# Even and odd channel tiles as the two halves of a seven-product matrix scheme, with other buffers for the first weight blocks of a layer

## Chip, cores and metric

The kernel runs on 1 core of one Trainium2 chip, as one program that takes all inputs of one inference step and writes all outputs. The metric is the device time of one execution in microseconds (us); lower is better. Before the change the median of 3 runs is 1267.34 us (1266.87 to 1272.12).

## What is computed

A trunk of two layers with width 1024 works on 544 tokens (512 of a prompt, 32 sampled) with shared weights. Layer 0 mixes by a causal convolution beside an attention, layer 1 by a chunked spatial gate; each layer then adds a squared-ReLU MLP of hidden width 4096. The change lies where a mixer's output projection ends and the MLP begins:

```python
xp = xp + merged @ wo                       # layer 0: output projection
xp = xp + mix_p                             # layer 1: (u * mix) @ w_out
xp = xp + sq_relu_mlp(rms_norm(xp, norm_ffn_g[layer]), w_ff_up[layer], w_ff_down[layer])

def sq_relu_mlp(h, w_up, w_down):
    a = jax.nn.relu(h @ w_up)
    return (a * a) @ w_down
```

All is float32.

## The kernel before

**Numbers in two parts.** Each float32 operand x is split into a rounded part "hi" and the rest "lo" = x - hi, and a product is three matmuls: hi by hi, lo by hi, hi by lo. ACT makes hi by a copy, DVE makes lo by a subtraction. Activations stand transposed: channels on the partitions, in KT = 8 channel tiles of 128, with T = 544 tokens in the free dimension, handled as two halves of HALF = 272.

**Output projection.** Eight output tiles (N_OUT = 20 to 27 in layer 0, N_OUTC = 44 to 51 in layer 1) are made by PE in function tile, 48 matmuls each, in two pairs of PSUM banks that take turns. A tile needs the lo part of its weights (lo_done) and, for its banks, the evacuation of the tile two before it (evac_done). DVE's add_to_x adds the tile to xT. The weight blocks are 256 columns wide (two tiles) and lie in two buffers of w_raw.

**Seven products for the up projection.** For a pair of hidden tiles (128 + 128 columns) the product of the 1024 channels with the tokens is treated as a product of 2 by 2 blocks: the channels are two halves (KH = 4 channel tiles each), the tokens are two halves, the hidden columns are two tiles. Seven products p1 to p7 of 12 matmuls take the place of eight. They need sums of weight blocks, which DVE makes in place (weight_sum: s1, s2, s3, s4), and sums of activation blocks: B_hi and B_lo (for p1, p2, p3, p5) and the three tiles of B_T (for p6, p7, p4). The halves are channel tiles 0 to 3 and 4 to 7.

**One layer's MLP.** The hidden width is cut into CHUNKS = 4 chunks of 1024. A chunk has 28 products (list ORDER: p1 0, p5 0, p1 1, p5 1, p2 0, p2 1, p6 0, p6 1, p7 0, p7 1, p4 0, p3 0, ...), then 16 halves of the down projection (d0, d1 for each of 8 output tiles). The weights of product q go to a ring of RING = 8 slots: ACT's weights_hi runs eight products ahead of PE, DVE's weights_lo seven. Between the products DVE also evacuates the results (part_11, part_22, part_12) and makes the lo parts of the hidden values (lo_row1, lo_row2), and ACT does relu and square. Product p6 0 waits for the evacuation of p1 0 and p2 0 by part_11 (c11_done).

**The stretch from projection to MLP.** Function to_ffn, once on ACT and once on DVE, goes through the eight output tiles j = 0 to 7. For j below 4 ACT makes B_hi of the first token half, and DVE the difference xg_f of the two token halves, from which ACT and DVE make the second half of B_hi and B_lo (p5's operand). For j of 4 and above, the operands of p6, p7 and p4 are made too: each combines channel tile j with channel tile j - 4. In the same loop come the splits of the last projection tiles (split_hi, split_lo), a running sum of squares for the norm (square_sum), the first sums of weights, and the first seven weights_lo. The norm's reciprocal, r_all, is made after the statistics in four parts (invert_part), at the products in INVERT_AT.

**What sets the order.** Every engine has one instruction queue, written by hand in the order of its block in the program, and semaphore waits between them. No scheduler moves anything. The weight loads are issued by SP (SyncE) in its own order, each behind the wait for its buffer. A block of the MLP's weights is 1 MB, loaded as two DMAs; block f of a layer goes to buffer f % 3: two buffers of w_raw, which it shares with the projections, and w_raw2, which lies where the mixer's data were.

Of the kernel before, what the change touches and what calls it, by code (L numbers as in the profile page):

```python
# [84 lines left out]
def build(nc, i, o):  # L85
# [78 lines left out]
    with ExitStack() as ctx:  # L164
# [187 lines left out]

        def raw_block(f):

            return w_raw[:, f % 3, :, :] if f % 3 < 2 else w_raw2[:, :, :]

        def raw_part(layer, c, product):

            name, u = product
            raw = raw_block(block_of(layer, c, product))  # L360
            if name[0] == "d":
                k0, col = KH * int(name[1]), P * (u % 2)
            else:
# [2060 lines left out]
```

## Time and profile before

| | before |
|---|---|
| median of 3 runs | 1267.34 us |
| the profiled execution, its own time | 1266.53 us |
| its span in the trace | 1264.8 us |
| PE busy | 1204.1 us, 95% of the span |
| DVE busy | 857.4 us, 68% |
| ACT busy | 604.2 us, 48% |
| GpSimd (POOL) busy | 64.7 us, 5% |
| chain of waits that ended last | PE 80%, DVE 11%, ACT 4%, issue 2%, DMA 1% |
[...]

How to read it: the profiled execution took 0.8 us less than the median, and 1.7 us of it lie outside the span of its instructions. A difference that is worked out in the trace is taken off 1266.53. PE is busy nearly all the time, so time can be won only where it stands or runs at the lower clock; the stretches in which it does are found in the timeline of PE by the idle time printed in brackets, with the instruction that is taken to have ended it. An instruction's printed duration holds some of its tail: where instructions follow one another without a gap, the distance from start to start is what each costs its engine.

### The profile page before, as it was taken

To read this page: it belongs to the slowest core of one execution; us is meant where nothing else is said; L and a number is where in the kernel's file an instruction comes from. 1 tells how busy PE (TensorE), PEld (TensorE's weight loads), DVE (VectorE), ACT (ScalarE), POOL (GpSimd) and SP (SyncE) were. 2 spreads that over 40 slices of the span, in tenths; PEclk is the share of its full clock that TensorE was granted. 3 is DMA by queue.
4 is the path that set the end of the run, shared out by engine and by line. 5 is a ranking of instruction groups with operands and counts; after the bars stand their busy time and mean duration, and the time that the engine had idled before them with its cause. 6 is when DMAs were issued, how large, how long until landed. Compare 5 with 4: busy or idle time off the path is not lost.

```text
span 1264.8 us, 23179 instructions
## 1 busy us (share of the span) xinstructions
PE 1204.1 (95%) x9394; PEld 1161.9 (92%) x9394; DVE 857.4 (68%) x1416; ACT 604.2 (48%) x1174; POOL 64.7 (5%) x111
## 2 busy tenths in 40 slices
PE   6999998889889999999999999989899999999998
PEld 5999885659889999999999999989899999999998
DVE  5798888655786585685686635668875755856852
ACT  5636655544465264264274434635551652642641
POOL 4010300000000000000000032030000000000000
PEclk9999997989989999999999999999899999999999
DMA  5431320243224124133141133222242241241312
GB/s 158 103 107 47 94 93 36 100 151 101 68 67 150 51 74 161 34 123 111 35 158 50 60 101 101 67 72 68 67 134 67 68 151 50 74 161 34 121 48 72
DMA packets 111777, 113.41 MB, mean 90 GB/s; under 512 B 6430, under 2 KB 105898, under 8 KB 111663
## 3 DMA queue, kind: packets, MB, share of 16 engines
q1 hardware_dynamic: 110111, 107.50, 26.7%
q0 software_dynamic: 1472, 4.41, 1.2%
q8 instruction: 75, 1.23, 0.4%
q14 instruction: 31, 0.25, 0.1%
q10 hardware_dynamic: 88, 0.02, 0.0%
HBM read 107.18 MB, written 5.16 MB: 89 GB/s over the span
## 4 chain that ended last, share of the span: by engine, by line
PE 80%; DVE 11%; ACT 4%; issue 2%; DMA 1%; POOL 1%; SPq 0%; ACTq 0%; DVEq 0%
PE ps L1224 30%; PE ps L1200 23%; PE ps L787 16%; PE ps L1026 5%; DVE w_lo L2161 2%; PE ps L939 1%; DMA w_raw<-in_w_in_ab 1%; DVE c_f L1880 1%; PE ps L969 1%; DVE w_lo L1791 1%; DVE r_all L2277 1%; PE ps L986 1%; POOL A_lo L761 1%; PE ps L951 1%; DVE ssq L1805 1%
## 5 line engine op out<-in xcount | busy, mean ns | idle before, releaser
L1585 ACT ACTIVATE w_hi<-w_raw 128x512 fp32r<-128x512 f32 x320 | 197.0, 625 | 232.5 <-PE ps L1224 178.0
L2161 DVE TENSOR_TENSOR w_lo<-w_raw,w_hi 128x512 fp32r<-128x512 f32 x320 | 213.8, 683 | 13.5 <-ACT w_hi L1585 13.3
L1224 PE MATMUL ps<-A_hi,w_hi 128*128 128x272 f32 x1024 | 212.1, 288 | 0.0
L1224 PE MATMUL ps<-A_lo,w_hi 128*128 128x272 f32 x1024 | 212.0, 288 | 0.0
L1224 PE MATMUL ps<-A_hi,w_lo 128*128 128x272 f32 x1024 | 211.2, 288 | 0.0
L2319 DVE TENSOR_TENSOR t_f<-ps,r_all 128x544 f32<-128x544 f32 x64 | 46.4, 724 | 170.7 <-PE ps L1224 170.7
L1224 PEld LDWEIGHTS ps<-A_hi,w_hi 128*128 128x128 f32 x1024 | 161.0, 188 | 0.1
L1224 PEld LDWEIGHTS ps<-A_hi,w_lo 128*128 128x128 f32 x1024 | 160.9, 188 | 0.0
L1224 PEld LDWEIGHTS ps<-A_lo,w_hi 128*128 128x128 f32 x1024 | 159.9, 189 | 0.0
L1200 PE MATMUL ps<-B_hi,w_hi 128*128 128x272 f32 x512 | 147.6, 288 | 3.7 <-DVE xT L2122 2.7
L1200 PE MATMUL ps<-B_hi,w_lo 128*128 128x272 f32 x512 | 147.6, 288 | 0.0
L1200 PE MATMUL ps<-B_lo,w_hi 128*128 128x272 f32 x512 | 147.3, 288 | 0.0
L1200 PE MATMUL ps<-t_h,w_hi 128*128 128x272 f32 x384 | 114.0, 297 | 12.7 <-DVE w_lo L2161 10.5
L1200 PE MATMUL ps<-t_l,w_hi 128*128 128x272 f32 x384 | 113.1, 294 | 0.0
L1200 PE MATMUL ps<-t_h,w_lo 128*128 128x272 f32 x384 | 112.5, 293 | 0.0
L1200 PEld LDWEIGHTS ps<-B_hi,w_hi 128*128 128x128 f32 x512 | 96.4, 188 | 4.4 <-issue 2.9
L1200 PEld LDWEIGHTS ps<-B_hi,w_lo 128*128 128x128 f32 x512 | 96.3, 188 | 0.0
L1200 PEld LDWEIGHTS ps<-B_lo,w_hi 128*128 128x128 f32 x512 | 96.3, 188 | 0.0
L787 PE MATMUL ps<-A_hi,w_hi 128*128 128x272 f32 x384 | 81.4, 293 | 9.8 <-DVE xT L1823 3.9
L1200 PEld LDWEIGHTS ps<-t_h,w_hi 128*128 128x128 f32 x384 | 74.5, 194 | 13.6 <-DVE w_lo L2161 10.9
L1880 DVE SCALAR_TENSOR_TENSOR c_f<-glu_p,conv_wT,c_f 128x512 f32<-128x512 f32 x120 | 83.4, 741 | 0.2
L787 PE MATMUL ps<-A_hi,w_lo 128*128 128x272 f32 x384 | 79.7, 289 | 0.0
(328 smaller groups left out, 2425.1 us busy)
## 6 DMA issues: line engine op xcount, KB each, us to landing
w_raw<-in_w_ff_up SPq DMA_DIRECT2D x64, 512.0 KB, 4.7
w_raw<-in_w_ff_down SPq DMA_DIRECT2D x64, 512.0 KB, 5.0
w_raw<-in_w_in_ab SPq DMA_DIRECT2D x20, 512.0 KB, 4.8
w_raw<-in_w_in_c SPq DMA_DIRECT2D x16, 512.0 KB, 4.5
w_raw<-in_w_out_ab SPq DMA_DIRECT2D x8, 512.0 KB, 5.3
k_pg<-in_cache_k SPq DMA_DIRECT2D x16, 256.0 KB, 4.3
v_pg<-in_cache_v SPq DMA_DIRECT2D x16, 256.0 KB, 3.9
w_raw<-in_w_out_c SPq DMA_DIRECT2D x8, 512.0 KB, 4.5
```

What stands on the lines that cost most here:

```text
L761: pool.tensor_tensor(A_lo[:, k, :], a_f[:, k % 2, :], A_hi[:, k, :].bitcast(F32), ALU.subtract)\
L787: mm = pe.matmul(ps[:, 2 * s + half, 0:HALF], wt[:, j % 4, k, :], mv[:, k, half * HALF:(half + 1) * HALF], start=(k == 0 and at_ == 0), st ...
L939: pe.matmul(ps[:, bank, 0:n], qT[0:HD + 2, h, NS + P * q:NS + P * q + P], kT[0:HD + 2, h, NS:NS + n], start=True, stop=False, skip_group_c ...
L951: mm = pe.transpose(ps[:, 4 + s % 2, P * j:P * j + P], prob[:, s % 3, P * j:P * j + P], ident[:, :])
L969: mm = pe.matmul(ps[HD * even:HD * even + HD, 7, P * q:P * q + P], v_nat[:, 1 + j, HD * h:HD * h + HD], pT[(2 * t + even) % 6][:, P * j:P ...
L1026: mm = pe.matmul(nat_ps(m), mv[:, k, c0:c0 + P], wt[:, s:s + 2, k, :], start=(k == 0 and at_ == 0), stop=(k == KT - 1 and at_ == 2))
L1200: mm = pe.matmul(ps[:, product_bank((name, u)), 0:HALF], wt[:, k, :], mv[:, k, :], start=(name in ("p1", "p2", "p5") and k == 0 and at_ == 0),
L1224: mm = pe.matmul(down_banks(u)[:, half, :], wt[:, k % KH, :], mv[:, k, half * HALF:(half + 1) * HALF], start=(k == 0 and at_ == 0), stop=( ...
L1585: act.activation(ring(w_hi, q), half_source(q), ACT.Copy).then_inc(fh_done, 1)
L1880: dve.scalar_tensor_tensor(out=c_f[:, c, NS:T], in0=glu_p[:, c, tap:tap + S], scalar=conv_wT[:, c, tap:tap + 1], in1=c_f[:, c, NS:T], op0= ...
L2161: dve.tensor_tensor(ring(w_lo, q), half_source(q), ring(w_hi, q).bitcast(F32), ALU.subtract)\
L2319: dve.tensor_tensor(two(t1_f[:, 1, :]), down_banks(j), two(r_all[:, :]), ALU.mult).then_inc(dn_evac, 1)
```

## The change

Seven edits go together.

1. The two channel halves of the seven-product scheme are the even and the odd channel tiles (k = 0, 2, 4, 6 and 1, 3, 5, 7) instead of the first and the last four. Weights are read as `raw[:, odd:KT:2, ...]`, activations as `B_hi[:, odd:KT:2, ...]`. The down projection keeps its halves.
2. In to_ffn an even j does what j below 4 did, an odd j what the others did; the operands of p6, p7 and p4 combine tile j with tile j - 1. Within an odd j all three differences are made before the lo parts.
3. In to_ffn DVE's split_lo of tile n0 + 3 stands ahead of the loop, and the others at the end of the step before the one they stood in. The first weights_lo stand at j = 4 to 7 (two each, one at 7) instead of j = 5 to 7, ACT's weights_hi at j = 4 to 7 at the end of the step.
4. The weight sums s1, s3 of pairs 0 and 1 go from j = 3 and 4 to j = 2 and 4, s2 of both pairs from p5 1 to p2 0 and p2 1.
5. The layer's first MLP block goes to w_raw2, whose wait is for the mixer's end, instead of w_raw; the next two go to w_raw, with waits for the lo parts of six and of eight projection tiles. In layer 1 the two buffers of w_raw swap roles, and so do those of the mixer's projections (tile_slot).
6. The first block of layer 1's mixer is loaded after d1 3 of the last chunk instead of d1 5.
7. Two of the four parts of the reciprocal move behind the up products of a layer's first chunk.

The diff, without the helper functions for slots and arrival counts:

```diff
         def raw_slot(f):
+            layer, m = f // (BLOCKS * CHUNKS), f % (BLOCKS * CHUNKS)
+            return (2, layer, 1 - layer)[m % 3]
...
-            return raw[:, k0:k0 + KH, col:col + P]
+            odd, col = {"p1": (0, 0), "p6": (0, 0), "p2": (1, 0), "p3": (1, 0), "p7": (0, P), "p4": (1, P)}[name]
+            return raw[:, odd:KT:2, col:col + P]
...
-            return B_hi[:, k0:k0 + KH, c0:c0 + HALF], B_lo[:, k0:k0 + KH, c0:c0 + HALF]
+            return B_hi[:, odd:KT:2, c0:c0 + HALF], B_lo[:, odd:KT:2, c0:c0 + HALF]
...   SP
-                            if f % 3 < 2:
-                                sp.wait_ge(lo_done, (N_OUT, N_OUTC)[layer] + 6 + 2 * (f % 3))
+                            if m > 0:
+                                sp.wait_ge(lo_done, (N_OUT, N_OUTC)[layer] + 4 + 2 * m)
...
-                    sp.wait_ge(fl_done, half_at(0, CHUNKS - 1, ("d1", 5 + 2 * m)) + 1)
+                    sp.wait_ge(fl_done, half_at(0, CHUNKS - 1, ("d1", 3 + 4 * m)) + 1)
...   PE, first product of a layer
-                            pe.wait_ge(xl_done, KT * (2 * layer + 1) + k + 1 + (KH if name == "p2" else 0))
+                            pe.wait_ge(xl_done, KT * (2 * layer + 1) + 2 * k + {"p1": 1, "p2": 2}[name])
...   ACT, x_operands
-                if j < KH:
-                    act.activation(xg_f[:, j, :], xT[:, j, :], ACT.Copy, scale=scale)
+                if j % 2 == 0:
+                    act.activation(xg_f[:, k, :], xT[:, j, :], ACT.Copy, scale=scale)
...
-                    for q in (2 * k, 2 * k + 1):
-                        weights_hi(layer * CHUNKS * HALVES + q)
-                    x_square(j, index)
...
+                    act.wait_ge(td_done, done + 4)
+                    act.activation(B_T["p4"][0][:, k, :], u2_f[:, k % 2, :], ACT.Copy).then_inc(th_done, 1)
                     x_square(j, index)
...   ACT, to_ffn
                     if j < 4:
                         split_hi(j, n0 + j + 4)
+                    else:
+                        for q in (2 * j - 8, 2 * j - 7):
+                            weights_hi(layer * CHUNKS * HALVES + q)
...   DVE
-                if (name, u) == ("p5", 1):
-                    weight_sum(layer, c, "s2", 0)
-                    weight_sum(layer, c, "s2", 1)
+                if name == "p2" and u < 2:
+                    weight_sum(layer, c, "s2", u)
...   DVE, to_ffn
+                split_lo(3, n0 + 3)
                 for j in range(8):
                     add_to_x(j, n0 + j, j % 2)
-                    if j < 5:
-                        split_lo(j + 3, n0 + j + 3)
-                    if j in (3, 4):
-                        weight_sum(layer, 0, "s1", j - 3)
-                        weight_sum(layer, 0, "s3", j - 3)
...
+                        if j == 2 or j == 4:
+                            weight_sum(layer, 0, "s1", j // 2 - 1)
+                        dve.wait_ge(th_done, done + 1)
...
+                        if j == 2 or j == 4:
+                            weight_sum(layer, 0, "s3", j // 2 - 1)
...
-                        if j >= 5:
-                            weights_lo(q0 + 2 * (j - 5))
-                            weights_lo(q0 + 2 * (j - 5) + 1)
-                        if j == 7:
-                            weights_lo(q0 + 6)
...
                     if j >= 2:
                         square_sum(j - 1, index)
-
-            INVERT_AT = (("p2", 3), ("p5", 3), ("p6", 2), ("p6", 3))
+                    if j < 4:
+                        split_lo(j, n0 + j + 4)
+                    else:
+                        weights_lo(q0 + 2 * j - 8)
+                        if j < 7:
+                            weights_lo(q0 + 2 * j - 7)
+
+            INVERT_AT = (("p2", 3), ("p5", 3))
...   DVE, ffn_chunk
                 for u in range(TAIL, HALVES):
+                    if c == 0 and u == TAIL:
+                        invert_part(layer, 2)
+                        invert_part(layer, 3)
```

Three places in the instruction order. On DVE in layer 0, from add_to_x of the last output tile (xT<-ps,xT); B_lo, t_l and xg_f are operands of the products, w_lo a weights_lo, w_raw<-w_raw a weight sum. Before:

```order
L2122 TENSOR_TENSOR xT<-ps,xT 128x544
L2202 SCALAR_TENSOR_TENSOR xg_f<-xT,vec,xg_f 128x272
L2206 SCALAR_TENSOR_TENSOR B_lo<-xT,vec,B_hi 128x544
L2210 TENSOR_TENSOR t_l<-xg_f,t_h 128x272
L2161 TENSOR_TENSOR w_lo<-w_raw,w_hi 128x512 x3
L2152 TENSOR_TENSOR w_raw<-w_raw 128x4x128
L2217 SCALAR_TENSOR_TENSOR xg_f<-xT,vec,xg_f 128x272
L2221 SCALAR_TENSOR_TENSOR u_f<-xT,vec,xg_f 128x272
L2225 TENSOR_TENSOR t_l<-xg_f,t_h 128x272
L2228 TENSOR_TENSOR t_l<-u_f,t_h 128x272
L1805 TENSOR_TENSOR ssq<-ssq,sq 128x544
L2161 TENSOR_TENSOR w_lo<-w_raw,w_hi 128x512
```

The same place on DVE after the change:

```order
L2135 TENSOR_TENSOR xT<-ps,xT 128x544
L2212 SCALAR_TENSOR_TENSOR xg_f<-xT,vec,xg_f 128x272
L2215 SCALAR_TENSOR_TENSOR xg_f<-xT,vec,xg_f 128x272
L2219 SCALAR_TENSOR_TENSOR u_f<-xT,vec,xg_f 128x272
L2223 SCALAR_TENSOR_TENSOR B_lo<-xT,vec,B_hi 128x544
L2227 TENSOR_TENSOR t_l<-xg_f,t_h 128x272
L2230 TENSOR_TENSOR t_l<-xg_f,t_h 128x272
L2233 TENSOR_TENSOR t_l<-u_f,t_h 128x272
L1818 TENSOR_TENSOR ssq<-ssq,sq 128x544
L2174 TENSOR_TENSOR w_lo<-w_raw_148,w_hi 128x512
L2165 TENSOR_TENSOR w_raw_148<-w_raw_148 128x4x128
L2174 TENSOR_TENSOR w_lo<-w_raw,w_hi 128x512
```

Three xg_f and u_f differences now stand together ahead of B_lo, and of the three w_lo in the middle one is left, behind the sum of squares; the rows behind these, down to the first part_11 (TENSOR_REDUCE), are a sum, two w_lo, a sum of squares and a w_lo in both.

On DVE late in the up products of layer 0's first chunk, around the last parts of the reciprocal (A_lo is a lo_row, t_f<-ps an evacuation). Before:

```order
L2161 TENSOR_TENSOR w_lo<-w_raw,w_hi 128x512
L2277 RECIPROCAL r_all<-r_all 128x136
L2161 TENSOR_TENSOR w_lo<-w_raw,w_hi 128x512
L2277 RECIPROCAL r_all<-r_all 128x136
L2250 TENSOR_REDUCE t_f<-ps 128x272
L2161 TENSOR_TENSOR w_lo<-w_raw,w_hi 128x512
```

And where these two parts stand after the change, at the end of the up products:

```order
L2276 TENSOR_TENSOR A_lo<-a_f,A_hi 128x544
L2271 TENSOR_TENSOR A_lo<-a_f,A_hi 128x544
L2276 TENSOR_TENSOR A_lo<-a_f,A_hi 128x544
L2174 TENSOR_TENSOR w_lo<-w_raw,w_hi 128x512
L2288 RECIPROCAL r_all<-r_all 128x136 x2
L2174 TENSOR_TENSOR w_lo<-w_raw,w_hi 128x512
L2333 TENSOR_TENSOR t_f<-ps,r_all 128x544
```

The two parts left the place ahead of the evacuation of p7 2 (TENSOR_REDUCE, part_22) and stand behind the last lo_row, ahead of the first evacuation of the down projection.

On SP in layer 0, from the last block of the output projection; each wait is the one ahead of that DMA, w_raw_148 is w_raw2. Before:

```order
L482 DMA w_raw<-in_w_out_ab 128x4x256
L596 DMA w_raw<-in_w_ff_up 128x4x256 [waits lo_done]
L596 DMA w_raw<-in_w_ff_up 128x4x256
L596 DMA w_raw<-in_w_ff_up 128x4x256 [waits lo_done]
L596 DMA w_raw<-in_w_ff_up 128x4x256
L596 DMA w_raw_148<-in_w_ff_up 128x4x256 [waits v_stored,spv_done]
```

After:

```order
L495 DMA w_raw<-in_w_out_ab 128x4x256
L609 DMA w_raw_148<-in_w_ff_up 128x4x256 [waits v_stored,spv_done]
L609 DMA w_raw_148<-in_w_ff_up 128x4x256
L609 DMA w_raw<-in_w_ff_up 128x4x256 [waits lo_done]
L609 DMA w_raw<-in_w_ff_up 128x4x256
L609 DMA w_raw<-in_w_ff_up 128x4x256 [waits lo_done]
```

The load that waits for v_stored and spv_done, third before, is first now; the two that wait for lo parts come behind it.

## Rows read from the trace of the kernel before

**Rows 1.** Busy time by stretch: start:end, length, PE, PEld, DVE, ACT, POOL, clock

```profile
337.30:393.49 56.19, 46.41 (x344) 45.43 (x343) 49.93 (x83) 33.77 (x67) 0.00 (x0) 0.94 0.29 92
441.60:483.85 42.25, 42.25 (x339) 42.25 (x338) 34.39 (x56) 28.19 (x54) 0.00 (x0) 1.00 0.38 120
882.30:935.55 53.25, 46.60 (x344) 45.84 (x343) 46.72 (x78) 31.11 (x62) 0.00 (x0) 0.94 0.30 98
```

**Rows 2.** Timeline of PE, layer 0: start, us, instruction, [idle before <-releaser]

```profile
331.22 0.49 PE L787 MATMUL ps<-A_hi,w_hi 128*128 128x272 f32 x2 [1.69 <-DVE xT L2122]
...
344.81 0.36 PE L1200 MATMUL ps<-B_hi,w_hi 128*128 128x272 f32 x1 [2.70 <-DVE xT L2122]
...
355.81 0.56 PE L1200 MATMUL ps<-t_h,w_hi 128*128 128x272 f32 x1 [5.24 <-DVE w_lo L2161]
...
387.22 0.36 PE L1200 MATMUL ps<-t_h,w_hi 128*128 128x272 f32 x1 [1.12 <-DVE t_f L2250]
```

**Rows 3.** Chain of work that ended last, both layers: start, us, what

```profile
355.81 8.27 PE ps L1200 x48
364.08 0.92 PE ps L796 x4
...
897.31 8.82 PE ps L1200 x48
```

**Rows 4.** Timeline of DVE, layer 0: the first weight sum of step j = 4

```profile
324.77 0.69 DVE L2141 TENSOR_TENSOR w_s<-w_raw 128x512 f32<-128x512 f32 x1 [5.37 <-DMA w_raw<-in_w_ff_up]
```

**Rows 5.** Timeline of DVE, layer 1: steps j = 4 to 7, to part_11

```profile
864.51 0.72 DVE L2122 TENSOR_TENSOR xT<-ps,xT 128x544 f32<-128x544 f32 x1 [0.48 <-PE ps L787]
...
871.86 0.72 DVE L2122 TENSOR_TENSOR xT<-ps,xT 128x544 f32<-128x544 f32 x1
...
878.05 0.72 DVE L2122 TENSOR_TENSOR xT<-ps,xT 128x544 f32<-128x544 f32 x1
...
885.45 0.71 DVE L2122 TENSOR_TENSOR xT<-ps,xT 128x544 f32<-128x544 f32 x1
886.20 0.50 DVE L2202 SCALAR_TENSOR_TENSOR xg_f<-xT,vec,xg_f 128x272 f32<-128x272 f32 x1
886.99 0.79 DVE L2206 SCALAR_TENSOR_TENSOR B_lo<-xT,vec,B_hi 128x544 fp32r<-128x544 f32 x1 [0.28 <-ACT B_hi L1601]
...
888.04 1.89 DVE L2161 TENSOR_TENSOR w_lo<-w_raw,w_hi 128x512 fp32r<-128x512 f32 x3
...
896.50 0.71 DVE L2242 TENSOR_REDUCE t_f<-ps 128x272 f32<-128x544 f32 x1
```

**Rows 6.** Timeline of DVE, layer 0, step j = 2

```profile
305.52 0.72 DVE L2122 TENSOR_TENSOR xT<-ps,xT 128x544 f32<-128x544 f32 x1 [2.27 <-PE ps L787]
306.16 1.22 DVE L1791 TENSOR_TENSOR w_lo<-w_raw,w_hi 128x1024 fp32r<-128x1024 f32 x1
307.47 0.50 DVE L2188 SCALAR_TENSOR_TENSOR B_lo<-xT,vec,B_hi 128x272 fp32r<-128x272 f32 x1
...
308.82 0.44 DVE L2194 TENSOR_TENSOR B_lo<-xg_f,B_hi 128x272 fp32r<-128x272 f32 x1 [0.50 <-ACT B_hi L1596]
309.18 0.72 DVE L1805 TENSOR_TENSOR ssq<-ssq,sq 128x544 f32<-128x544 f32 x1
```

**Rows 7.** Timeline of ACT, layer 0, step j = 2

```profile
306.93 0.51 ACT L1593 ACTIVATE B_hi<-xT,vec 128x272 fp32r<-128x272 f32 x1
```

**Rows 8.** Timeline of DVE, layer 1: last part of the reciprocal

```profile
927.38 1.00 DVE L2277 RECIPROCAL r_all<-r_all 128x136 f32<-128x136 f32 x1
```

**Rows 9.** Timelines ahead of layer 1's output projection: DVE, then POOL

```profile
835.52 1.78 DVE L2397 TENSOR_TENSOR a_f<-u_f,v_f 128x544 f32<-128x544 f32 x1 [0.60 <-POOL A_lo L761]
...
838.07 1.33 POOL L761 TENSOR_TENSOR A_lo<-a_f,A_hi 128x544 fp32r<-128x544 f32 x1 [1.35 <-ACT A_hi L1772]
```

**Rows 10.** Timeline of DVE, a later chunk: w_lo from w_raw and from w_s1

```profile
455.86 0.68 DVE L2161 TENSOR_TENSOR w_lo<-w_raw,w_hi 128x512 fp32r<-128x512 f32 x1
...
457.70 0.68 DVE L2161 TENSOR_TENSOR w_lo<-w_s,w_hi 128x512 fp32r<-128x512 f32 x1
```

More of the change, by code:

```diff
@@ L351, in down_banks, with tile_slot, tile_arrived, raw_slot @@
             return ps[:, 6:8, 0:HALF] if u % 2 == 0 else ps[:, 3:5, 0:HALF]
+        def tile_slot(n):
+            return (n // 2 + (n >= N_INC)) % 2
+        def tile_arrived(n):
+            return raw_in[tile_slot(n)], 32 * (n // 4 + 1 + (FF_LOADS[tile_slot(n)] if n >= N_INC else 0))
+        def raw_slot(f):
+            layer, m = f // (BLOCKS * CHUNKS), f % (BLOCKS * CHUNKS)
+            return (2, layer, 1 - layer)[m % 3]
         def raw_block(f):
-            return w_raw[:, f % 3, :, :] if f % 3 < 2 else w_raw2[:, :, :]
+            return w_raw[:, raw_slot(f), :, :] if raw_slot(f) < 2 else w_raw2[:, :, :]
         def raw_part(layer, c, product):
@@ L386, in operand @@
                 return B_T[name][0][:, :, :], B_T[name][1][:, :, :]
-            k0, c0 = {"p1": (0, 0), "p2": (KH, 0), "p3": (KH, HALF), "p5": (0, HALF)}[name]
-            return B_hi[:, k0:k0 + KH, c0:c0 + HALF], B_lo[:, k0:k0 + KH, c0:c0 + HALF]
+            odd, c0 = {"p1": (0, 0), "p2": (1, 0), "p3": (1, HALF), "p5": (0, HALF)}[name]
+            return B_hi[:, odd:KT:2, c0:c0 + HALF], B_lo[:, odd:KT:2, c0:c0 + HALF]
         def item(s):
@@ L1195, in product @@
                         if name in ("p1", "p2"):
-                            pe.wait_ge(xl_done, KT * (2 * layer + 1) + k + 1 + (KH if name == "p2" else 0))
-                        else:
-                            pe.wait_ge(tl_done, 4 * KH * layer + (k + 1 if name == "p5" else KH + 3 * k + {"p6": 1, "p7": 2, "p4": 3}.get(name, 0)))
+                            pe.wait_ge(xl_done, KT * (2 * layer + 1) + 2 * k + {"p1": 1, "p2": 2}[name])
+                        elif name != "p3":
+                            pe.wait_ge(tl_done, 4 * KH * layer + 4 * k + {"p5": 1, "p6": 2, "p7": 3, "p4": 4}[name])
                     for wt, mv, at_ in ((w_h, b_h, 0), (w_l, b_h, 1), (w_h, b_l, 2)):
@@ L1320, in split_hi @@
             def split_hi(j, n):
-                b = j // 2
-                act.wait_ge(raw_in[b % 2], 32 * (n // 4 + 1 + (FF_LOADS if n >= N_INC else 0)))
-                act.activation(w_hi[:, j % 4], w_raw[:, b % 2, :, P * (j % 2):P * (j % 2) + P], ACT.Copy)\
+                act.wait_ge(*tile_arrived(n))
+                act.activation(w_hi[:, j % 4], w_raw[:, tile_slot(n), :, P * (j % 2):P * (j % 2) + P], ACT.Copy)\
                    .then_inc(hi_done, 1)
@@ L1790, in split_lo @@
                 dve.wait_ge(hi_done, n + 1)
-                dve.tensor_tensor(w_lo[:, j % 4, :, :], w_raw[:, (j // 2) % 2, :, P * (j % 2):P * (j % 2) + P],
+                dve.tensor_tensor(w_lo[:, j % 4, :, :], w_raw[:, tile_slot(n), :, P * (j % 2):P * (j % 2) + P],
                                   w_hi[:, j % 4, :, :].bitcast(F32), ALU.subtract).then_inc(lo_done, 1)
@@ L2176, in to_ffn @@
                 n0, gain, index, q0 = (N_OUT, N_OUTC)[layer], V_FFN[layer], 2 * layer + 1, layer * CHUNKS * HALVES
+                split_lo(3, n0 + 3)
                 for j in range(8):
                     add_to_x(j, n0 + j, j % 2)
[L2179 to L2183 removed]
                     scale = vec[:, gain + j:gain + j + 1]
[L2185 to L2186 removed]
+                    k, done = j // 2, 4 * KH * layer + 4 * (j // 2)
+                    if j % 2 == 0:
                         dve.wait_ge(xh_done, KT * index + j + 1)
@@ L2204, in to_ffn @@
                            .then_inc(td_done, 1)
+                        dve.scalar_tensor_tensor(out=xg_f[:, k, HALF:T], in0=xT[:, j, HALF:T], scalar=scale,
+                                                 in1=xg_f[:, k, HALF:T], op0=ALU.mult, op1=ALU.subtract)\
+                           .then_inc(td_done, 1)
+                        dve.wait_ge(td_done, done + 2)
+                        dve.scalar_tensor_tensor(out=u2_f[:, k % 2, :], in0=xT[:, j, 0:HALF], scalar=scale,
+                                                 in1=xg_f[:, k, 0:HALF], op0=ALU.mult, op1=ALU.subtract)\
+                           .then_inc(td_done, 1)
                         dve.wait_ge(xh_done, KT * index + j + 1)
```

57 lines of the change are left out of this document (21 added, 36 removed).

## The prediction

> **What bounds the kernel now.** I read the page's busy table first: PE works 95% of the span, so only stretches where it stands or runs slow can give time. Then the chain of waits: long unbroken PE pieces, and two thickets of DVE, ACT and PE pieces, one in each layer, between the output projection and the second half of the first chunk's up products. Then the table of stretches. An undisturbed up phase (28 products of 12 matmuls) takes 42.25 us with PE busy throughout, so a product takes 1.51 us and 48 matmuls 6.04. The first up phase of a layer takes 56.19 us in layer 0 and 53.25 in layer 1 [rows 1]. It also holds the statistics, 0.92 [rows 3], so its ideal is 43.17: 13.0 us are lost in layer 0 and 10.1 in layer 1. Layer 0 loses 1.69 more within the projection, where a tile waits for the evacuation of an earlier one [rows 2]. At most 24.8 us can be won here.
>
> Where the loss lies, in layer 0 [rows 2]: 2.70 idle before p5 1, 5.24 before p6 0, 1.12 before p4 2, the rest in shorter pieces. Behind the longest idle stretch the clock is at its lower level: the 48 matmuls of p6 and p7 take 8.27 us in layer 0 and 8.82 in layer 1 [rows 3] against 6.04, so 2.2 and 2.8 more; the mean clock of the phase is 0.94 in both [rows 1]. The trace puts the long wait down to a w_lo, but that w_lo (of p6 0) was long done. What ends just ahead of PE's start is the TENSOR_REDUCE of part_11: in layer 1 it starts at 896.50, ends at 897.21 [rows 5], and PE starts at 897.31 [rows 3]. It is late only because of DVE's queue: add_to_x of the last tile starts at 885.45. Tile 4 is added on time at 864.51 and PE makes a tile in 6.01 us, so tile 7 could be added at 882.54; DVE is 2.9 us late there, and needs 11.76 more to the end of part_11 [rows 5].
>
> Layer 0 has another cause on top. At j = 4 DVE stands 5.37 us for the second MLP block [rows 4], whose load waits on SP for the split of the last projection tile. The idle 1.69 and 2.70 of PE name add_to_x, which stood behind that wait.
>
> **The change, part by part.**
>
> *Even and odd halves.* DVE's heavy steps (three B_T operands) are j = 1, 3, 5, 7 instead of 4 to 7. The count of instructions is the same; what changes is how much is left when tile 7 comes. Step lengths on DVE, from add to next add:
> - Even step: 4.3 us from the add at 305.52 to the end of the sum of squares (309.18 + 0.64) [rows 6]. The split_lo inside is replaced by nothing, but B_lo starts no earlier: it needs ACT's B_hi, which ends at 307.44, and it starts at 307.47 now [rows 6, 7]. With two w_lo (three take 1.89 [rows 5], so 0.63 each) it is 5.6. At j = 4 two weight sums of about 0.6 are added, one of which fills the 0.50 wait for ACT: 6.3. At j = 6 two sums stand behind: 6.8.
> - Odd step: step 5 takes 6.19 now (871.86 to 878.05), with its two w_lo [rows 5]. The differences now stand ahead of B_lo, so the wait for ACT's B_hi (0.28, with the wake-up about 0.4) is covered: 5.8.
> - For j below 4 a split_lo of 1.22 [rows 6] stands where the two w_lo do, so these steps are no longer than 6.3 either and are caught up by the next.
>
> So j = 4 starts on time, j = 5 is 0.3 late, j = 6 0.1, and j = 7 0.9 late instead of 2.9. From there to the end of part_11 it is 11.76 less two of the three w_lo (1.26) and less the covered wait (0.4): 10.1. The end of part_11 comes 2.0 + 1.7 = 3.7 us earlier, 893.5 in the times of layer 1, and PE resumes at 893.6. PE is ready at 882.31 + 6 x 1.51 = 891.4: of the six products ahead only the two p2 need the whole of tile 7, and they begin four products (6 us) after its end, when DVE, 0.9 late, has long made its B_lo, the fifth instruction of the step. New wait: 2.2 us per layer. Its bounds are 0, if DVE's waits vanish altogether, and the 5.25 of now; I take 2.2, worked from rows of the same stretch.
>
> *The clock.* Idle stretches of 1.69 and 2.70 us are followed by full speed, that of 5.24 by the lower level [rows 2, 3]. With 2.2 us I count no loss, so the 2.2 and 2.8 us go.
>
> *Two parts of the reciprocal moved.* They take 1.0 each [rows 8] and stand ahead of the part_22 whose end frees p4 2; without them it is 2 us earlier and the 1.12 idle us go. At their new place they are hidden by the down projection: DVE is seven products (21 us) ahead there, and the first use of r_all comes after a whole down tile of 6 us. Nothing on SP or POOL passes them. Cost if that cover failed: 2 us per layer.
>
> *First block to w_raw2, lo parts a tile sooner.* The wait of 5.37 us for the load goes [rows 4]: block 0 is issued right behind the last projection block and first used at j = 2; block 1 waits for six lo parts, which are done at the end of step 1, two whole tiles (12 us) before its sums at j = 4. With it go 1.69 and the 2.70 in layer 0. SP holds nothing else behind these waits. In layer 1 the load was already in time, and I count nothing for it, nor for the first mixer block of layer 1, whose split still waits for d1 4.
>
> *split_lo ahead of the loop.* In layer 0 DVE idles there. In layer 1 it falls beside POOL's last A_lo, on which PE waits. DVE's product a_f took 1.78 us beside a POOL subtraction, against 0.72 for a sum of the same size [rows 6, 9]: they hold each other up. Now DVE would start split_lo at 837.30 and be at it until 838.5, and POOL's A_lo, which started at 838.07 [rows 9], would start 0.45 later. Between 0 (DVE alone is held up) and 1.2 (a whole split_lo) I take 0.45, the time that both want to work. [...]
>
> *Strided reads.* Blocks with a distance of 2 KB between their four runs of 512 bytes are read instead of 1 KB. A w_lo from w_raw (1 KB apart) and one from w_s1 (contiguous) both take 0.68 [rows 10], so I count nothing; the other end is a rival.
>
> **The sum.** First up phase: 43.17 + 2.2 = 45.4. Layer 0 gains 56.19 - 45.4 + 1.69 = 12.5. Layer 1 gains 53.25 - 45.4 - 0.45 = 7.4. Together 19.9, taken off the profiled execution's 1266.53 (0.8 below the median, less than the range): **1246.6 us**.
>
> **The rivals.**
>
> *The clock still falls in the new wait.* Several short waits stand close together there. Against it: 1.69 and 2.70 in layer 0 did no harm [rows 2]. Price 2.2 + 2.8 [rows 3]: 1251.6. [...]
>
> *DVE is not relieved.* If the hand-offs between DVE and ACT in the even steps (two per step, B_hi and its second half) cost what the moved work saves, part_11 is as late as now, with the low clock behind: per layer 5.25 and 2.2 or 2.8 stay instead of 2.2. That takes 5.3 and 5.9 from the gains: 1257.8. For it speaks that DVE is 49.93 of 56.19 us busy [rows 1]; against it, that the steps above come out no longer than a tile.
>
> *The load is no earlier.* If block 0 or 1 still came late in layer 0 (two blocks now load at once), DVE's 5.37 stays: 1246.6 + 5.4 = 1252.0.
>
> *Slower: the strided reads cost.* 24 w_lo and 16 weight sums per chunk read with the wider stride, in all eight chunks. DVE is busy 34.39 of 42.25 us in an undisturbed up phase [rows 1], so it has 7.9 us to spare: from 0.2 us more per instruction PE starts to wait. From 0.26 the gain of 19.9 is eaten (40 x 0.26 - 7.9 = 2.5, times 8). At half as long again (0.34): 40 x 0.34 - 7.9 = 5.7, times 8 = 46 us, 1292. Against it: rows 10.
>
> **How the numbers follow.** Forecast 0.70, its own range 1242.2 (no new wait) to 1250 (a wait of nearly 4). Clock rival 0.09, DVE not relieved 0.09, late load 0.06, strided reads 0.06. The range 1241.5 to 1254 holds the forecast, the clock and the late load, 0.85, less their tails. Half a percent, about what a measurement of this kernel can tell from no change, is 6.3 us; the first four cases lie further below 1267.34 than that. Faster 0.92, no difference 0.03, slower 0.05 (the last two share the strided reads and what I did not think of).
>
> **What would show it.** In the changed profile the first up phases should be near 45.4 us in both layers, with one idle stretch of about 2 us of PE before p6 0 and full clock behind it; no DMA as releaser of DVE in the projection of layer 0; no idle PE before p4 2; add_to_x of the last tile within 1 us of its tile; w_lo at 0.68. Wrong would be: the later chunks longer than 42.25 (strided reads), a lower clock behind p6 0, or PE idle over 4 us there (DVE's queue).

## The result, and the profile after

The changed kernel takes 1247.18 us (median of 4 runs, 1246.38 to 1250.94); the kernel before takes 1267.22 us beside it (4 runs, 1266.87 to 1272.12). The ratio is 0.9844, 95% interval [0.9827, 0.9861]. Forecast were 1246.6 us. The profiled execution took 1246.93 us, 19.6 less than the one of before, with a span of 1245.2 us and a mean granted clock of 0.990 (0.985 before).

To see where the 19.6 us lie, the two spans are cut at the same places of the program: start and end of the output projection of layer 0, end of the first up phase, the last wait for POOL ahead of the projection of layer 1, its end, end of the first up phase there. The kernel before, by stretch (start:end, length, then busy time of PE, PEld, DVE, ACT and POOL, granted clock, DMA share, GB/s); the two first up phases between these stretches stand in [rows 1]:

```profile
290.18:337.30 47.12, 45.42 (x360) 45.19 (x360) 28.48 (x48) 19.30 (x34) 2.47 (x7) 1.00 0.35 112
393.49:839.46 445.97, 441.52 (x3498) 438.31 (x3496) 281.50 (x418) 201.01 (x336) 29.83 (x27) 1.00 0.26 84
839.46:882.31 42.85, 42.85 (x343) 42.85 (x343) 31.59 (x54) 21.98 (x39) 0.41 (x1) 1.00 0.32 102
935.55:1264.80 329.25, 323.81 (x2584) 323.18 (x2583) 199.57 (x318) 140.64 (x260) 0.00 (x0) 0.99 0.26 85
```

The same stretches of the changed kernel, with the first up phases, and a later up phase at the end:

```profile
289.59:334.79 45.20, 45.20 (x361) 45.20 (x361) 34.38 (x61) 22.61 (x41) 2.47 (x7) 1.00 0.35 117
334.79:379.88 45.09, 43.39 (x343) 43.05 (x341) 41.29 (x69) 30.39 (x59) 0.00 (x0) 1.00 0.35 114
379.88:826.17 446.29, 441.62 (x3498) 438.42 (x3496) 284.65 (x421) 201.20 (x337) 30.06 (x27) 1.00 0.25 84
826.17:870.66 44.49, 44.49 (x342) 44.49 (x343) 33.28 (x60) 22.53 (x41) 0.42 (x1) 0.96 0.30 98
870.66:915.75 45.09, 43.39 (x342) 43.05 (x341) 41.27 (x69) 30.38 (x59) 0.00 (x0) 1.00 0.35 113
915.75:1245.20 329.45, 323.94 (x2586) 323.31 (x2584) 201.57 (x320) 140.75 (x261) 0.00 (x0) 1.00 0.26 85
...
428.16:470.39 42.23, 42.23 (x338) 42.23 (x338) 34.40 (x56) 28.15 (x54) 0.00 (x0) 1.00 0.36 120
```

| stretch | before | after | won |
|---|---|---|---|
| start to the projection of layer 0 | 290.18 | 289.59 | 0.6 |
| projection of layer 0 | 47.12 | 45.20 | 1.9 |
| first up phase, layer 0 [rows 1] | 56.19 | 45.09 | 11.1 |
| to the last wait for POOL | 445.97 | 446.29 | -0.3 |
| projection of layer 1 behind it | 42.85 | 44.49 | -1.6 |
| first up phase, layer 1 [rows 1] | 53.25 | 45.09 | 8.2 |
| to the end | 329.25 | 329.45 | -0.2 |
| sum | | | 19.6 |

The gain lies where it was expected, in the two first up phases and the projection of layer 0. One row is not what was expected: the projection of layer 1 is busy throughout in both kernels, but takes 1.6 us more, at a mean clock of 0.96. The experiments come back to it. Nothing in the first row was edited; its 0.6 us are spread (below).

What is left of the idle stretches of [rows 2], from the timeline of PE of the changed kernel (start, length, instruction, idle before it and what ended that):

```profile
345.74 0.36 PE L1213 MATMUL ps<-t_h,w_hi 128*128 128x272 f32 x1 [1.70 <-DVE w_lo L2174]
...
826.17 0.52 PE L800 MATMUL ps<-A_hi,w_hi 128*128 128x272 f32 x2 [1.89 <-POOL A_lo L774]
...
881.61 0.36 PE L1213 MATMUL ps<-t_h,w_hi 128*128 128x272 f32 x1 [1.70 <-DVE w_lo L2174]
```

1.70 us ahead of p6 0 in each layer is all the idle time of its up phase. The 1.69 in the projection, the 2.70 ahead of p5 1 and the 1.12 ahead of p4 2 are gone. In the chain of waits (start, length, what) the 48 matmuls behind the wait, 8.27 and 8.82 us in [rows 3], run at full speed:

```profile
345.74 6.29 PE ps L1213 x48
...
826.17 38.65 PE ps L800 x294
...
881.61 6.29 PE ps L1213 x48
```

The middle line is the slower projection of layer 1; the same 294 matmuls take 37.12 us when the clock stays up (e7, below).

DVE in layer 0, from its timeline: a weight sum w_s of j = 2, the adds (xT) of steps 4 to 7, a B_lo of j = 6 that waits for ACT, and the first part_11 (TENSOR_REDUCE):

```profile
307.65 0.69 DVE L2154 TENSOR_TENSOR w_s<-w_raw 128x512 f32<-128x512 f32 x1
...
316.95 0.72 DVE L2135 TENSOR_TENSOR xT<-ps,xT 128x544 f32<-128x544 f32 x1 [0.37 <-PE ps L800]
...
323.07 0.72 DVE L2135 TENSOR_TENSOR xT<-ps,xT 128x544 f32<-128x544 f32 x1
...
327.46 0.68 DVE L2174 TENSOR_TENSOR w_lo<-w_raw,w_hi 128x512 fp32r<-128x512 f32 x1
...
328.98 0.72 DVE L2135 TENSOR_TENSOR xT<-ps,xT 128x544 f32<-128x544 f32 x1 [0.24 <-PE ps L800]
330.93 0.50 DVE L2196 SCALAR_TENSOR_TENSOR B_lo<-xT,vec,B_hi 128x272 fp32r<-128x272 f32 x1 [1.23 <-ACT B_hi L1606]
...
335.69 0.72 DVE L2135 TENSOR_TENSOR xT<-ps,xT 128x544 f32<-128x544 f32 x1
...
344.92 0.71 DVE L2253 TENSOR_REDUCE t_f<-ps 128x272 f32<-128x544 f32 x1
```

The sum that waited 5.37 us for its load [rows 4] has no wait. The last add starts at 335.69, 0.90 behind the end of its tile (334.79); before, in layer 1, it was 885.45 against 882.31, 3.14 behind [rows 1, 5]. From that add to the end of part_11 it is 344.92 + 0.71 - 335.69 = 9.94 us (11.76 before), and PE starts at 345.74.

### The profile page after: what moved, and what is told of

It reads as the page before. It is cut to its first block, busy times and chain, and to the rows that moved or that the text cites. A ratio compares the mean times of both kernels' runs of the same rounds, so it can differ in the third digit from the quotient of the medians.

```text
span 1245.2 us, 23181 instructions
## 1 busy us (share of the span) xinstructions
PE 1199.5 (96%) x9394; PEld 1158.6 (93%) x9394; DVE 856.1 (69%) x1416; ACT 604.3 (49%) x1174; POOL 64.9 (5%) x111
## 4 chain that ended last, share of the span: by engine, by line
PE 86%; DVE 7%; ACT 3%; issue 2%; DMA 1%; POOL 1%; SPq 0%; ACTq 0%; DVEq 0%
PE ps L1237 31%; PE ps L1213 26%; PE ps L800 18%; PE ps L1039 5%; PE ps L952 1%; DMA w_raw<-in_w_in_ab 1%; DVE c_f L1893 1%; PE ps L982 1%; PE ps L999 1%; POOL A_lo L774 1%; PE ps L964 1%; DVE a_f L2411 1%; DVE w_lo L2174 1%; DVE w_lo L1804 0%; PE ps L1100 0%
## 5 line engine op out<-in xcount | busy, mean ns | idle before, releaser
L1237 PE MATMUL ps<-A_lo,w_hi 128*128 128x272 f32 x1024 | 212.1, 289 | 0.0
L800 PE MATMUL ps<-A_lo,w_hi 128*128 128x272 f32 x384 | 80.6, 292 | 0.0
```

Of the source, the lines that this page charges most:

```text
L800: mm = pe.matmul(ps[:, 2 * s + half, 0:HALF], wt[:, j % 4, k, :], mv[:, k, half * HALF:(half + 1) * HALF], start=(k == 0 and at_ == 0), st ...
L1237: mm = pe.matmul(down_banks(u)[:, half, :], wt[:, k % KH, :], mv[:, k, half * HALF:(half + 1) * HALF], start=(k == 0 and at_ == 0), stop=( ...
```

## The experiments

Times of e1 to e4 stand beside one set of runs of the kernel before (median 1268.83), e5 and e6 beside another on the same chip (1267.78), e7 and e8 together beside a third on another chip (1267.96). The runs of one kernel spread over 3 to 10 us, so the verdicts rest on stretches of the profiles more than on medians. Since the start of layer 0's projection alone lies between 289.21 (e3) and 292.69 us (e1) in these profiles, with nothing edited ahead of it, spans are compared only after that is looked at.

### e1: the buffers alone

The kernel before with edits 5 and 6:

```diff
+            layer, m = f // (BLOCKS * CHUNKS), f % (BLOCKS * CHUNKS)
+            return (2, layer, 1 - layer)[m % 3]
...
-                            if f % 3 < 2:
-                                sp.wait_ge(lo_done, (N_OUT, N_OUTC)[layer] + 6 + 2 * (f % 3))
+                            if m > 0:
+                                sp.wait_ge(lo_done, (N_OUT, N_OUTC)[layer] + 4 + 2 * m)
...
-                    sp.wait_ge(fl_done, half_at(0, CHUNKS - 1, ("d1", 5 + 2 * m)) + 1)
+                    sp.wait_ge(fl_done, half_at(0, CHUNKS - 1, ("d1", 3 + 4 * m)) + 1)
```

> The kernel before with only the other buffers, load waits and the earlier load of layer 1's first mixer block (edits 5 and 6); halves, order on DVE and reciprocal as before. Theory (the layers lose time to DVE's queue, layer 0 also to the late load): DVE's 5.37 us wait for the load in layer 0 goes, with it PE's idle 1.69 and 2.70; layer 0's first up phase becomes like layer 1's, 53.25 instead of 56.19 us; 5.2 us of idle PE ahead of p6 0 and the lower clock behind it stay in both layers. Gain 1.69 + 2.94 = 4.6: 1261.9 us. Rival (the late load is what made part_11 late, the even and odd order adds little): layer 0 gains all it gained with the whole change, 12 us: 1254.

Measured: 1260.68 us (1260.15 to 1262.91), ratio 0.9933 [0.9911, 0.9956]. Its first up phases by stretch, and the idle time of PE in them:

```profile
337.91:389.94 52.03, 45.40 (x343) 44.64 (x341) 46.70 (x78) 30.94 (x62) 0.00 (x0) 0.97 0.31 99
879.02:931.76 52.74, 46.09 (x342) 45.33 (x341) 46.70 (x78) 30.94 (x62) 0.00 (x0) 0.94 0.29 97
```

```profile
352.89 0.57 PE L1215 MATMUL ps<-t_h,w_hi 128*128 128x272 f32 x1 [5.25 <-DVE w_lo L2175]
...
383.84 0.36 PE L1215 MATMUL ps<-t_h,w_hi 128*128 128x272 f32 x1 [1.12 <-DVE t_f L2264]
...
894.00 0.56 PE L1215 MATMUL ps<-t_h,w_hi 128*128 128x272 f32 x1 [5.26 <-DVE w_lo L2175]
```

In its chain of waits, the 48 matmuls behind the long wait in layer 0 and in layer 1:

```profile
352.89 7.80 PE ps L1215 x48
...
894.00 8.51 PE ps L1215 x48
```

DVE no longer waits for a load in layer 0, and that layer looks like layer 1 now: 4.2 us less than 56.19, the 2.70 ahead of p5 1 gone, and of the 0.72 ahead of p2 0, one product later, 0.26 left (0.28 in layer 1 before). The wait ahead of p6 0 stays as long as it was (5.25 against 5.24), and so does the one ahead of p4 2. With 1.9 us in the projection layer 0 gains 6.1 us, more than the 4.6 expected, mostly since the matmuls behind the same wait lose less here: 7.80 us, where 8.82 of layer 1 before were counted on. So the load delayed layer 0's projection and p5 1, and the order of DVE's own work delays p6 0.

### e2: the halves without the buffers

The changed kernel with the buffers of before (edits 5 and 6 undone, the diff of e1 the other way round):

```diff
-            layer, m = f // (BLOCKS * CHUNKS), f % (BLOCKS * CHUNKS)
-            return (2, layer, 1 - layer)[m % 3]
+            return f % 3
```

> The changed kernel with buffers, load waits and the mixer's load as before (without edits 5 and 6). Theory: the early steps on DVE now want the blocks sooner than the old waits let SP load them, in both layers. Block 0 waits for six lo parts (end of step 1, 304.2 in the times of layer 0) and takes 5.4 us: DVE, which wants it at 307.7, stands 2.0; block 1 waits for eight (end of step 3) and DVE stands about 2.3 more at step 4. The last add_to_x comes some 4 us later, PE stands about 6 instead of 1.9 us around p5 1 and p6 0, and the lower clock follows it (2.2 to 2.8): 6 to 7 us per layer, 1259 to 1261; 1255 if the clock holds. Rival (the load matters in layer 0 alone, as the trace of before has it in time in layer 1): only layer 0 loses, 1253.

Measured: 1253.07 us (1251.07 to 1256.72), ratio 0.9884 [0.9857, 0.9911]. The theory is refuted for layer 1 and the rival right: only layer 0 loses, with waits of DVE near the 2.0 and 2.3 us expected there. The two first up phases by stretch, then the waits of DVE in layer 0, then PE:

```profile
335.23:385.53 50.30, 45.03 (x342) 44.49 (x341) 44.60 (x75) 32.20 (x63) 0.00 (x0) 0.97 0.32 101
874.80:919.89 45.09, 43.39 (x342) 43.04 (x341) 41.29 (x69) 30.39 (x59) 0.00 (x0) 1.00 0.35 112
```

```profile
310.01 0.69 DVE L2151 TENSOR_TENSOR w_s<-w_raw 128x512 f32<-128x512 f32 x1 [1.84 <-DMA w_raw<-in_w_ff_up]
...
324.24 0.69 DVE L2151 TENSOR_TENSOR w_s<-w_raw 128x512 f32<-128x512 f32 x1 [2.57 <-DMA w_raw<-in_w_ff_up]
```

```profile
340.80 0.36 PE L1210 MATMUL ps<-B_hi,w_hi 128*128 128x272 f32 x1 [0.87 <-DVE xT L2132]
...
349.99 0.56 PE L1210 MATMUL ps<-t_h,w_hi 128*128 128x272 f32 x1 [4.40 <-DVE w_lo L2171]
```

Both first blocks come late in layer 0, at j = 2 and j = 4, and DVE carries the delay along to the last tile, whose add starts 4.7 us behind its tile (339.93 against 335.23) instead of 0.90: PE's idle time grows from 1.70 to 0.87 + 4.40 and the clock falls behind it (7.70 us for the 48 matmuls). That is 5.2 us for layer 0. Layer 1 takes 45.09 us, as in the changed kernel. The mistake was to take the buffer numbers per layer: in the kernel before, f in f % 3 runs on over both layers, a layer has 32 blocks, and 32 % 3 = 2, so block 0 of layer 1 already went to w_raw2. (The description of the kernel above says "block f of a layer"; it is the block's number over both; so edit 5 gives the first block another buffer in layer 0 alone.) What the prediction said, that the load is in time there already, stands, and this is the reason.

### e3: two parts of the reciprocal put back

```diff
-            INVERT_AT = (("p2", 3), ("p5", 3))
+            INVERT_AT = (("p2", 3), ("p5", 3), ("p6", 2), ("p6", 3))
...
-                    if c == 0 and u == TAIL:
-                        invert_part(layer, 2)
-                        invert_part(layer, 3)
```

> The changed kernel with the last two parts of the reciprocal back among the up products (without edit 7). Theory: the part_22 that frees p4 2 comes 2 us later, PE stands 1.1 to 1.2 us ahead of p4 2 in both layers, and nowhere else: plus 2.3, 1249.2 us. Rival (DVE's lead after the change absorbs two parts): no idle PE there, 1246.9.

Measured: 1250.82 us (1249.05 to 1255.15), ratio 0.9868 [0.984, 0.9897]; span 1247.3, 2.1 more than the changed kernel. Each first up phase takes 46.44 us instead of 45.09, and the wait ahead of p4 2 is back in both layers:

```profile
374.79 0.36 PE L1213 MATMUL ps<-t_h,w_hi 128*128 128x272 f32 x1 [1.11 <-DVE t_f L2261]
...
911.81 0.36 PE L1213 MATMUL ps<-t_h,w_hi 128*128 128x272 f32 x1 [1.11 <-DVE t_f L2261]
```

So edit 7 is worth 1.35 us per layer. At its new place it costs nothing that shows: the stretch from there to the last wait for POOL takes 446.32 us in e3 and 446.29 in the changed kernel.

### e4: the first lo parts one step later

The seven weights_lo of a layer's first products at j = 5 to 7 (two, two, three), where the kernel before has them, all else as changed:

```diff
-                    else:
-                        weights_lo(q0 + 2 * j - 8)
-                        if j < 7:
-                            weights_lo(q0 + 2 * j - 7)
+                    elif j > 4:
+                        weights_lo(q0 + 2 * j - 10)
+                        weights_lo(q0 + 2 * j - 9)
+                        if j == 7:
+                            weights_lo(q0 + 6)
```

> The changed kernel with the first seven weights_lo at steps 5 to 7 (2, 2, 3, as before) instead of 4 to 7. Theory: the last add_to_x is on time, but two w_lo and two weight sums (4 x 0.6) more stand between it and part_11: its end comes 1.7 us later, PE's wait ahead of p6 0 grows from 1.7 to 3.4 us idle. If the clock holds over 3.4 us: plus 3.4, 1250.3. If it falls as it did behind 5.24 us: plus 5 more, 1255.3. Rival (the wait ahead of p6 0 is not set by the length of DVE's queue behind the last tile): wait unchanged, 1246.9.

Measured: 1252.64 us (1249.35 to 1259.83), ratio 0.9888 [0.9845, 0.9931], between the two cases. The profile shows why: in one execution both happened. The chain of waits, whose two lines are the 48 matmuls behind the wait ahead of p6 0 in layer 0 and in layer 1:

```profile
347.38 6.29 PE ps L1213 x48
...
883.48 7.80 PE ps L1213 x48
```

PE's idle time ahead of them is 3.41 and 3.42 us, as the two lines of its timeline say:

```profile
347.38 0.36 PE L1213 MATMUL ps<-t_h,w_hi 128*128 128x272 f32 x1 [3.41 <-DVE w_lo L2174]
...
883.48 0.36 PE L1213 MATMUL ps<-t_h,w_hi 128*128 128x272 f32 x1 [3.42 <-DVE w_lo L2174]
```

The wait came out at the 3.4 us expected. In layer 0 the last add is on time here (0.2 behind its tile, 334.91 against 334.71), but two weights_lo and the two weight sums that go with them stand in the last step, some 0.6 each: 2.4 more on the path and 0.7 less lateness make the 1.7 us of idle PE per layer that this part of edit 3 saves. The clock's answer to the same wait was full speed once and the lower level once, for 1.5 us.

### e5 and e6: what the remaining waits are worth

e5 takes part_11 of pairs 0 and 1 in front of the weights_lo that stand ahead of it in the first chunk; e6 is e5 with split_lo(3) of layer 1 behind the first add, out of the way of POOL's last A_lo:

```diff
-                    up_round(layer, c, *ORDER[u])
-                    if u < TAIL - 1:
-                        weights_lo(q0 + u + RING - 1)
+                    if not (c == 0 and ORDER[u] in (("p2", 0), ("p2", 1))):
+                        up_round(layer, c, *ORDER[u])
                     if c == 0 and ORDER[u] == ("p1", 1):
+                        part_11(layer, c, 0)
+                    if c == 0 and ORDER[u] == ("p5", 1):
+                        part_11(layer, c, 1)
                         square_sum(KT - 1, 2 * layer + 1)
+                    if u < TAIL - 1:
+                        weights_lo(q0 + u + RING - 1)
...   e6 alone
-                split_lo(3, n0 + 3)
+                if layer == 0:
+                    split_lo(3, n0 + 3)
                 for j in range(8):
                     add_to_x(j, n0 + j, j % 2)
+                    if j == 0 and layer == 1:
+                        split_lo(3, n0 + 3)
```

> The changed kernel with part_11 of pairs 0 and 1 in the first chunk of a layer put ahead in DVE's queue (behind the second and third w_lo of the chunk instead of the fourth and fifth; the last sum of squares and a w_lo go behind them). Same instructions. Theory: part_11 of pair 0 can start when p2 0 is done, 1.4 us before PE is through with p2 1, and nothing but its place in the queue holds it. Its end comes 1.2 to 1.9 us earlier, PE's 1.7 idle us ahead of p6 0 go in both layers, no other wait appears: minus 3.8, 1243.1 us, first up phase 43.3. Rival (DVE's work as a whole is the limit there): the wait moves to p6 1 or a p7 and the time stays 1246.9.

> The run with part_11 ahead, and in layer 1 the first split_lo of the output projection put back behind the first add_to_x, out of the way of POOL's last A_lo. Theory (DVE and POOL hold each other up): POOL's last A_lo takes 1.33 instead of 1.56 us and PE's wait for it 1.66 instead of 1.89: 0.2 us less than the run it is built on, 1242.9, to be seen in the trace only. Rival (POOL's 1.56 has another cause): both unchanged.

Measured: e5 1245.41 us (1243.21 to 1249.48), ratio 0.9826 [0.9806, 0.9846]; e6 1243.84 us (1243.40 to 1248.48), ratio 0.9824 [0.9806, 0.9841]. In e5 PE has no idle time in either first up phase, by stretch:

```profile
336.57:380.18 43.61, 43.61 (x343) 43.13 (x341) 40.94 (x69) 30.02 (x59) 0.00 (x0) 1.00 0.35 116
870.99:914.24 43.25, 43.25 (x343) 43.03 (x341) 41.10 (x69) 30.29 (x59) 0.00 (x0) 1.00 0.36 114
```

Together they are 3.3 us shorter than in the changed kernel (3.8 expected), and the rival, in which DVE's work as a whole is the limit, is out. The span is only 1.6 us shorter than the changed kernel's, since its projection of layer 0 starts 1.8 us later in that execution, ahead of anything edited. e6, by stretch, first up phases of layer 0 and 1:

```profile
334.80:378.54 43.74, 43.66 (x343) 43.13 (x341) 40.94 (x69) 29.93 (x59) 0.00 (x0) 1.00 0.35 111
869.02:912.28 43.26, 43.26 (x342) 43.03 (x341) 41.12 (x69) 30.28 (x59) 0.00 (x0) 1.00 0.36 117
```

Against the ideal of 43.17 that the prediction worked out, 0.1 to 0.6 us are left. Ahead of layer 1's projection, DVE's split_lo (w_lo) and the last A_lo of POOL in the changed kernel, then that A_lo in e6:

```profile
823.72 1.21 DVE L1804 TENSOR_TENSOR w_lo<-w_raw,w_hi 128x1024 fp32r<-128x1024 f32 x1
...
824.57 1.55 POOL L774 TENSOR_TENSOR A_lo<-a_f,A_hi 128x544 fp32r<-128x544 f32 x1 [1.35 <-ACT A_hi L1785]
```

```profile
823.25 1.33 POOL L774 TENSOR_TENSOR A_lo<-a_f,A_hi 128x544 fp32r<-128x544 f32 x1 [1.35 <-ACT A_hi L1785]
```

Without split_lo beside it POOL takes 1.33 us again, as in [rows 9], and PE waits 1.67 instead of 1.89 us. That is the price of that edit: 0.22 us.

### e7 and e8: the changed kernel and e6 on one chip

No edit: the two kernels once more, side by side.

> The changed kernel once more, beside e8 on the same chip, so that the two can be told apart by more than their distances from the kernel before. Expected: 1247.2 us, 0.984 of the kernel before, with 1.70 us of idle PE ahead of p6 0 in each layer.

> The version of e6 (part_11 of pairs 0 and 1 ahead, split_lo(3) of layer 1 behind the first add_to_x) once more, beside e7. Theory: the two waits of 1.70 us are paid by PE in full and the POOL wait is 0.2 shorter, so 2 x 1.70 + 0.2 = 3.6 us below e7, 1243.6 us. Rival: the gain seen between chips is their spread, and here the two are within 1 us.

Measured: e7 1248.53 us (1244.85 to 1250.44), ratio 0.9839 [0.9816, 0.9863]; e8 1243.81 us (1241.58 to 1251.08), ratio 0.9816 [0.9786, 0.9845]. The medians are 4.7 us apart where 3.6 were expected, but the intervals overlap. The spans are 1245.2 and 1242.2, and those of the first pair 1245.2 and 1241.7, so 3.0 and 3.5 us apart. That e6 is the faster one rests on both pairs and on its missing waits; how much, between 3 and 5 us, is open within this spread.

The second execution of the changed kernel also tells what the slow projection of layer 1 was. In e7 it takes:

```profile
827.76:870.71 42.95, 42.95 (x342) 42.95 (x343) 33.28 (x60) 22.56 (x41) 0.42 (x1) 1.00 0.31 101
```

And the 294 matmuls, 38.65 us in the first execution:

```profile
827.76 37.12 PE ps L800 x294
```

The same program, the same 1.89 us of waiting ahead of it, and the clock stays up: 42.95 against 44.49 us. The 1.5 us are not a cost that the change has in every execution. (The span is 1245.2 us all the same, as the projection of layer 0 starts 1.6 us later in e7, at 291.16.)

## Why the prediction was right, point by point

**The first up phase.** Forecast 45.4 us in both layers, measured 45.09 in both. Its statement that the loss is a matter of DVE's lateness at the last tile, and not of DVE's total work, is what e1, e4 and e5 bear out: the same work in another order gives 5.25, 3.41, 1.70 or no idle time ahead of p6 0.

**The step lengths.** Adds to adds in layer 0: j = 4 takes 6.12 us (323.07 - 316.95, forecast 6.3), j = 6 6.71 (6.8), j = 5 5.91 with the 0.24 of waiting at its end, so 5.7 (5.8). B_lo of the even steps starts 1.95 behind the add (330.93 - 328.98), as in [rows 6], still held by ACT. No step is longer than was worked out, so the rival in which DVE is not relieved is out. The last add was to be 0.9 late and is 0.67 (0.90 behind the tile's end, less the 0.23 of an add on time, which [rows 5] and PE's tile time gave). From it to the end of part_11: 9.94, forecast 10.1.

**The new wait.** Forecast 2.2, measured 1.70 in both layers. The term was too large by 0.5. The two smaller errors just named make 0.4 of that; the phase as a whole exceeds the ideal of 43.17 by 1.92, since PE also starts slowly behind the wait (6.29 us for 48 matmuls, against 6.04).

**The clock behind the wait.** Forecast full speed, measured 6.29 us in both layers of both executions of the changed kernel. The rival in which it falls did not come about there, but e4 shows how near it was: with 1.7 us more of idle time it fell once in two. Its price there was 1.5 us for 48 matmuls (7.80 against 6.29). The rival's 2.2 and 2.8 were reckoned from 6.04 us and behind waits of 5.24 and 5.25; against 6.29 such waits cost 1.5 to 2.5 (7.80 and 8.51 in e1, 8.27 and 8.82 in [rows 3]).

**The reciprocal.** The 1.12 us are gone; e3 gets them back by undoing that edit alone, with 0.2 more around them.

**The loads.** DVE's wait for the load is gone in layer 0, and with it 1.9 us in the projection (forecast 1.69). e1 and e2 show that in layer 0 neither edit does the other's work: without the new buffers DVE waits 1.84 + 2.57 us, without the new halves PE waits 5.25.

**Beside POOL.** Forecast 0.45, measured 0.22. DVE's split_lo starts at 823.72 and takes 1.21 us, as long as alone (1.22, [rows 6]); POOL's A_lo starts behind it, at 824.57, and takes 1.55 instead of 1.33 ([rows 9]; e6). Here POOL paid and DVE didn't. In the row behind the forecast it was the other way round: POOL's A_lo from 835.38 took 1.34 and kept its time, and DVE's a_f of [rows 9], which began at 835.52, took 1.78. The A_lo ahead of that one, from 833.53, took 1.89, beside an a_f that had begun at 833.49 and took 0.72. So in these three overlaps the one that started first kept its time and the other took longer; what lies behind it, the runs don't show. The two A_lo as a pair in the timeline of POOL before the change:

```profile
833.53 3.19 POOL L761 TENSOR_TENSOR A_lo<-a_f,A_hi 128x544 fp32r<-128x544 f32 x2 [1.35 <-ACT A_hi L1772]
```

The forecast's "they hold each other up" missed that. Of the size, 0.08 is explained, as split_lo starts 0.85 us ahead of POOL instead of the 0.77 worked out; the rest of the 0.23 too much stays open.

**The strided reads.** A w_lo takes 0.68 us, as in [rows 10], and a later up phase 42.23 (42.25, [rows 1]). That rival is out.

**The sum.** Layer 0: 11.10 + 1.92 = 13.0 (forecast 12.5). Layer 1: 8.16 - 0.22 = 7.9 (forecast 7.4). These are 21.0 us, 1.1 more than the 19.9 forecast: 0.3 in each up phase, 0.2 in layer 0's projection, 0.2 beside POOL. In the profiled execution 1.5 are given back to the clock in layer 1's projection, a term that the prediction did not have, and the rest (0.2 net) is the small change of the stretches in the table, not explained further. The mechanism is borne out stretch by stretch; that the total came within 0.6 us is partly luck, since the up phases erred to one side and the clock of layer 1's projection to the other.

## What to carry to other kernels

When an engine off the critical path must finish a chain behind the last tile, count its lateness at that tile, step by step, and move work to steps that have slack, though its total stays the same. Where the consumer waits behind several queued instructions, first ask which of them it really needs: here moving two evacuations ahead of weights that PE needs only later took 3.3 us off the two up phases (e5). Compare variants stretch by stretch, since a part that nobody edited can move by 3.5 us between executions and hide or feign an edit of that size.

## What the runs showed of the hardware that was not expected

**The clock is not decided by the length of one wait.** Idle time of PE ahead of p6 0, and the 48 matmuls behind it: 1.70 us, 6.29; 3.41 us, 6.29; 3.42 us, 7.80 (e4, both in one execution); 4.40 us, 7.70 (e2); 5.25 us, 7.80 and 5.26 us, 8.51 (e1, layers 0 and 1); 5.24 us, 8.27 [rows 2, 3] and 5.25 us, 8.82 (before, layers 0 and 1). PE had no other idle time in the 50 us ahead of each of e4's two waits, and no difference between them was found in the profile. When it falls differs too: behind 4.40 us and more the granted clock is 0.50 in the first 2 us of the matmuls and their first one takes 0.56 or 0.57 us. Behind e4's 3.42 us the first takes 0.36, as at full speed, and the clock is 0.73 in the stretch from 884 to 886 us and 0.50 from 886 to 888, when PE is busy again.

**Short waits together can do the same, or not.** Ahead of layer 1's projection PE waits for POOL three times within 5.3 us, 1.07, 0.29 and then 1.66 to 1.89 us. Of the ten profiled executions of this study, before and after among them, the clock stayed up behind it in five (before, e1, e2, e4, e7) and fell in five (after, e3, e5, e6, e8), which cost 1.3 to 1.5 us. After and e7 are one program with the same waits, and e6 and e8 another. The length of the third wait doesn't tell: with 1.88 or 1.89 us the clock fell in three of six executions, with 1.66 or 1.67 in two of four. A timeline of the clock in the changed kernel, by stretches of 2 us:

```profile
824.00:826.00 2.00, 0.28 (x3) 0.07 (x1) 0.93 (x1) 0.49 (x1) 1.43 (x1) 1.00 0.00 0
826.00:828.00 2.00, 1.83 (x12) 1.83 (x13) 0.72 (x1) 0.01 (x1) 0.59 (x2) 0.83 0.93 298
828.00:830.00 2.00, 2.00 (x11) 2.00 (x11) 0.82 (x2) 1.70 (x3) 0.00 (x0) 0.50 0.83 292
830.00:832.00 2.00, 2.00 (x15) 2.00 (x15) 1.00 (x3) 1.38 (x2) 0.00 (x0) 0.82 0.22 46
832.00:834.00 2.00, 2.00 (x18) 2.00 (x18) 0.70 (x1) 0.00 (x0) 0.00 (x0) 1.00 1.03 346
```

Here the clock goes to 0.50 when PE is already busy again, and is back at 1.00 from 832 us on. In e3 and e6 it is at 0.50 from the first 2 us behind the wait. So these waits had a price in two parts, their own length and, in five of the ten executions, 1.3 to 1.5 us behind them, for a reason that stays open; a prediction for this kernel should carry both.
